# Low parts of 32 weight tiles made in an earlier stage, kept in DRAM and loaded back

## The reference, cut to what matters

```python
def peer_ffn(x, w_q, sub_keys, expert_u, expert_v):
    ...
    def chunk(args):
        xc, ec, gc = args
        a = jnp.einsum('cd,ckd->ck', xc, expert_u[ec])
        w = (gc * jax.nn.gelu(a.astype(jnp.float32))).astype(x.dtype)
        return jnp.einsum('ck,ckd->cd', w, expert_v[ec])
```

## Time and profile before

| | us |
|---|---|
| median of 3 runs | 2193.26 (2191.37 to 2193.62) |
| the profiled execution, device time | 2191.22 |
| its span in the trace | 2189.5 |

### The profile page before, as it was taken

The page is one execution under the profiler, slowest core; times in us unless marked ns, Lnnn a source line. Parts: engine busy times, 40 slices in busy tenths (PEclk is TensorE's granted clock), DMA queues, the critical chain, the costliest instruction groups (busy, mean ns, idle before and its releaser), DMA issues.

```text
span 2189.5 us, 33425 instructions
## 1 busy us (share of the span) xinstructions
PE 2124.8 (97%) x11713; PEld 1787.7 (82%) x11713; DVE 1650.1 (75%) x3228; ACT 1042.0 (48%) x1940; POOL 638.7 (29%) x425
## 2 busy tenths in 40 slices
PE   7999999999999988899999989999999999999999
PEld 6888888888888545687899988999998888888777
DVE  6555555534367687564399999999988989999999
ACT  5333333322243477744455535999844333343332
POOL 0000000000040000020100223777626767777773
PEclk9999999999999999999999999999999999999999
DMA  5322222232234200022355888999989999999997
GB/s 195 97 86 86 86 86 95 80 99 98 98 101 177 77 1 1 1 68 87 125 177 177 279 260 290 382 408 400 392 306 408 419 418 418 418 418 418 411 418 290
DMA packets 137228, 484.57 MB, mean 221 GB/s; under 512 B 15056, under 2 KB 30416, under 8 KB 135184
## 3 DMA queue, kind: packets, MB, share of 16 engines
q1 hardware_dynamic: 75456, 229.93, 30.0%
q0 software_dynamic: 59056, 225.14, 26.1%
q10 hardware_dynamic: 2592, 27.85, 3.1%
HBM read 435.42 MB, written 46.92 MB: 220 GB/s over the span
## 4 chain that ended last, share of the span: by engine, by line
PE 63%; DVE 21%; DMA 10%; ACT 3%; issue 2%; POOL 1%; ACTq 0%; DVEq 0%; POOLq 0%
PE bank L495 15%; PE bank L496 15%; PE bank L497 15%; DMA rows<-peer_v,idxU 9%; PE bank L1257 7%; DVE rows L2327 6%; DVE wlo L482 4%; PE bank L510 2%; DVE own L2332 2%; DVE hot L2485 2%; DVE hot L2483 2%; PE bank L610 1%; PE bank L570 1%; PE bank L813 1%; PE bank L1211 1%
## 5 line engine op out<-in xcount | busy, mean ns | idle before, releaser
L495 PE MATMUL bank<-act_hi,whi 128*128 128x320 f32 (+1 forms) x1840 | 646.4, 351 | 23.2 <-DVE wlo L482 19.8
L496 PE MATMUL bank<-act_lo,whi 128*128 128x320 f32 (+1 forms) x1840 | 635.1, 345 | 0.0
L497 PE MATMUL bank<-act_hi,wlo 128*128 128x320 f32 (+1 forms) x1840 | 634.8, 345 | 0.0
L482 DVE TENSOR_TENSOR wlo<-raw,whi 128x1024 fp32r<-128x1024 f32 x398 | 485.8, 1222 | 141.5 <-ACT whi L478 139.3
L478 ACT ACTIVATE whi<-raw 128x1024 fp32r<-128x1024 f32 x398 | 416.4, 1055 | 262.5 <-PE bank L1257 114.1
L495 PEld LDWEIGHTS bank<-act_hi,whi 128*128 128x128 f32 x1840 | 346.0, 188 | 65.7 <-DVE wlo L482 23.4
L497 PEld LDWEIGHTS bank<-act_hi,wlo 128*128 128x128 f32 x1840 | 345.8, 188 | 32.7
L496 PEld LDWEIGHTS bank<-act_lo,whi 128*128 128x128 f32 x1840 | 346.2, 188 | 31.4 <-issue 0.7
L762 POOL DMA_INDIRECT rows<-peer_u,idxU x128 | 196.7, 1537 | 337.5 <-DVE udot L2327 168.9
L1257 PE MATMUL bank<-whi,h_hi 128*128 128x512 f32 x768 | 238.4, 391 | 7.1 <-DVE wlo L482 4.2
L1257 PE MATMUL bank<-whi,h_lo 128*128 128x512 f32 x768 | 237.4, 390 | 0.0
(11 more groups left out here) (403 smaller groups left out, 2905.6 us busy)
## 6 DMA issues: line engine op xcount, KB each, us to landing
raw<-tiles SPq DMA_DIRECT2D x398, 512.0 KB, 4.9
gates_dram<-stage ACTq DMA_DIRECT2D x12, 2048.0 KB, 11.6
wg<-gates_dram POOLq DMA_DIRECT2D x16, 1536.0 KB, 17.0
acts_dram<-gelu SPq DMA_DIRECT2D x120, 160.0 KB, 5.1
hf<-acts_dram POOLq DMA_DIRECT2D x30, 640.0 KB, 13.6
bias<-alibi POOLq DMA_DIRECT2D x16, 256.0 KB, 2.9
w1s<-cmp_w POOLq DMA_DIRECT2D x1, 4096.0 KB, 13.0
res<-x_t ACTq DMA_DIRECT2D x4, 512.0 KB, 6.9
```

The source lines that it names most:

```text
L482: dve.tensor_tensor(wlo[:, j.slot, :], raw[:, j.slot, :], whi[:, j.slot, :].bitcast(F32), ALU.subtract).then_inc(lo_made, 1)
L495: pe.matmul(to, wh, x, start=(kc == 0), stop=False)
L496: pe.matmul(to, wh, xl, start=False, stop=False)
L497: last = pe.matmul(to, wl, x, start=False, stop=(kc == KC - 1))
```

## The change

32 tiles of the up projection, those of U jobs 36 to 67 (`EARLY_LO`), get an additional job each in the merge stage. That stage goes from 32 to 64 jobs, in groups of four: two of its own (slots 0 and 1) and two of the additional ones (slots 2 and 3). For an additional job SP loads the raw tile, ACT makes the high part, DVE the low part, and SP stores the low part to `lo_dram` in DRAM; nothing is multiplied. DVE counts the job as done once its store has landed (`low_stored`). To keep the count in order, PE waits, ahead of the last chunk of the next group's first product, until the group's stored jobs are counted (`after_stored`).

In stage U DVE makes no low part for jobs 36 to 67: it waits for the high part and for `lo_moved`, and raises `lo_made`. SP loads the low part of job j + 4 right after it has stored the gelu of job j, first waiting until the load two before has landed (two semaphores in turn, so two are under way). It then asks for the raw tile of job j + 8 when the high part of job j + 4 is made, where it waited for its low part before. ACT makes all high parts as before.

Row dots are spread anew: tile 2 from 6 to 12, tile 3 from 18 to 28, gates from 76 to 72, rest from 12 to 18. So 130 uses lie ahead of stage V and 190 in it, where it was 112 and 208. `load_gates(0)` comes after the gather number `SEEN_GATES + ROWS + DOTS_REST // 4`. Some semaphores are renamed or shared.

```diff
-J_C = J_B + 32
+J_C = J_B + 64
...
+EARLY_LO = range(36, 68)
...
-DOTS_TILE = [(0, 0), (0, 0), (6, 10), (18, 0)]
-DOTS_GATES = 76
-DOTS_REST = 12
+DOTS_TILE = [(0, 0), (0, 0), (12, 10), (28, 0)]
+DOTS_GATES = 72
+DOTS_REST = 18
...
+            with sp.Fori(0, J_C // RING - J_B // RING) as i:
+                for m in range(RING):
+                    load(Job(J_B + RING + m, i))
+                    if m >= 2:
+                        sp.dma_start(lo_dram[bass.ds(i * 2 + m - 2, 1), :, :],
+                                     wlo[:, m, :].bitcast(F32)).then_inc(lo_moved[m % 2], 16)
...
-            with sp.Fori(0, U_REST // RING) as i:
+            def store_and_load(i, at_, with_lo):
                 for m in range(RING):
-                    j = Job(J_U + m, i)
+                    j = Job(J_U + at_ + m, i)
                     was_taken(sp, j)
-                    sp.dma_start(acts_dram[bass.ds(i * RING + m, 1), :, :], gelu[:, m, :])\
+                    sp.dma_start(acts_dram[bass.ds(i * RING + at_ + m, 1), :, :], gelu[:, m, :])\
                         .then_inc(acts_stored[m], 16)
-                    load(Job(J_U + 8 + m, i))
+                    if with_lo:
+                        moved = lo_moved[m % 2]
+                        sp.wait_ge(moved, (i * 2 + m // 2 + len(EARLY_LO) // 2) * 16)
+                        sp.dma_start(wlo[:, j.slot, :].bitcast(F32), lo_dram[bass.ds(i * RING + m, 1), :, :])\
+                            .then_inc(moved, 16)
+                        sp.wait_ge(hi_made, Job(J_U + at_ + RING + m, i).n + 1)
+                        into_raw(Job(J_U + at_ + 8 + m, i))
+                    else:
+                        load(Job(J_U + at_ + 8 + m, i))
...
-            for n in range(SEEN_GATES + ROWS + DOTS_REST // 2):
+            for n in range(SEEN_GATES + ROWS + DOTS_REST // 4):
                 gather(n)
...
+            def after_stored(j):
+                def wait(kc):
+                    if kc == KC - 1:
+                        result_of(pe, j)
+                return wait
...
+                    if m % 4 < 2:
+                        if m == 1:
+                            pe.wait_ge(y_split, 2 * KC)
+                        hi, lo = ((act_hi, act_lo), (yc_hi, yc_lo), (act_hi, act_lo), (ya_hi, ya_lo))[m // 4 % 2 * 2 + m % 4]
+                        multiply(pe, j, hi, lo, after_stored(Job(J_B - 1 + m, i, 16)) if m % 4 == 0 else None)
...
+                def low_stored(unit, *stored_jobs):
+                    for moved in lo_moved:
+                        dve.wait_ge(moved, (unit + 1) * 16)
+                    for j in stored_jobs:
+                        dve.wait_ge(taken[j.slot], j.turn + 1)
+                        dve.sem_inc(taken[j.slot], 1)
+                        dve.sem_inc(job_done, 1)
...
             def u_job(n):
-                make_lo(dve, Job(J_U + n).ahead())
+                j = Job(J_U + n).ahead()
+                if n + AHEAD in EARLY_LO:
+                    dve.wait_ge(hi_made, j.n + 1)
+                    at_ = n + AHEAD - EARLY_LO.start
+                    dve.wait_ge(lo_moved[at_ % 2], 16 * (len(EARLY_LO) // 2 + at_ // 2 + 1))
+                    dve.sem_inc(lo_made, 1)
+                else:
+                    make_lo(dve, j)
...
+    early = u[EARLY_LO.start:EARLY_LO.stop].reshape(16, 2, P, D)
+    b = np.concatenate([b.reshape(16, 2, P, D), early], 1).reshape(64, P, D)
```

132 lines of the change are left out of this document (78 added, 54 removed).

## The result

Before: 2192.94 us (median of 4 runs). After: **2242.87 us** (2241.09 to 2243.99, 4 runs), ratio 1.0229 with a 95% interval of 1.0216 to 1.0242. The change costs 50 us. The forecast was 2202, with a range to 2217: the sign was right, the size wrong.

The account below looks back on a forecast made before the run. PE bounds the kernel nearly everywhere, DVE tile 3. Merge stage 0, tiles 2 and 3 +14, gate steps -4.6, rest of U +3, stage V -4 sum to +8.4 us on 2193.26: 2201.7, likeliest 2202, range 2179 to 2217.

Parts of the forecast that it names:

- The gate steps, the rest and stage V: After the tiles: gate steps -4.6 us, rest of U +3, stage V -4, from row dots moved between them.
- The merge stage: 0 was forecast: Merge stage: additional loads, splits and stores cost 0 us, upper end +5, since transfers and DVE have room.
- its store has about 5 us to land, and a raw load lands in 3.4 us here: Merge stage: a group's second store has about 5 us to land, judged by a raw load's 3.4 us.
- DVE waits some 1.3 us per group, which its slack covers: Merge stage: at a loaded queue's landing time of 6.3 us, DVE's wait of 1.3 us per group fits its slack.
- the merge stage longer than 179 us: Merge stage: a sign that would show the forecast wrong; it expected still 174 us.
- Tiles 2 and 3: +14 was forecast: Tiles 2 and 3: 64.6 MB at 418 GB/s take 154.6 us, 9.6 more; with imperfect packing +14, ends -6 and +22.
- its 3.7 us: Start of tiles 2 and 3: 3.7 us of transfers lost because POOL's gathers begin only at 1228.
- at the other end the last jobs have no low load and DVE binds them as now: End of tile 3: DVE, not transfers, binds the last jobs; part of why the term was +14.
- the upper end I had given, +22: Tiles 2 and 3: upper end of the +14 term, if nothing is regained at the end either.
- The first (transfers fit, 0.25): Rival, tiles 2 and 3: low loads and rows find room, over 445 GB/s; total 2179.7 us; chance 0.25.
- The second (they cancel, 0.17): Rival: tiles lose only 3 to 8 us, sum within 3 us of zero, about 2193 us; chance 0.17.
- The third: Rival, jobs 40 to 67: SP's queue gets half the rate, 5.8 us per job, +64 us, 2251.7; chance 0.05.

Follow-up runs that it names:

- Experiment 2: Changed kernel with the low part's store issued ahead of the raw load in the merge stage: 2216.44 us, ratio 1.0112.
- experiment 10, second run: Kernel before plus the merge stage storing 32 low parts, store first, `mg_lo` ahead of the store wait, none loaded back: 2193.06 us, ratio 1.0000.
- experiment 11: Changed kernel with its own dots, store first, `mg_lo` ahead of the store wait, low-load wait on PE: 2210.02 us, ratio 1.0076.
- experiments 4 and 5: Changed kernel with row dots and gates load as before the change: alone 2233.05 us; with the store also ahead of the raw load 2201.60 us.
- experiment 6: Kernel before with only the change's row dots and place of `load_gates(0)`, no low parts stored or loaded: 2203.01 us, ratio 1.0047.
- experiment 13: Mended kernel, dots as before, low loads for jobs 52 to 67 only, first one ahead of the waiting raw load: 2192.28 us; for jobs 56 to 71: 2191.67 us.

## Why the prediction went wrong

**What was right.** That the transfers, not DVE, would bind tiles 2 and 3: 406 to 416 GB/s against the forecast 410 to 420, 20.3 us of PE waits for low loads in small pieces against "some 20 to 30", and 64.6 MB against 64.6 (378 GB/s for 171 us). Halving the loads took 13 us away, halving DVE's work on the dots 2. The gate steps, the rest and stage V were right in kind and size.

**The merge stage: 0 was forecast, 24.2 measured, and 4.8 more behind it.** The step that failed is "its store has about 5 us to land, and a raw load lands in 3.4 us here", with the bound "DVE waits some 1.3 us per group, which its slack covers". The landing time came from a queue in which each load goes out alone. The store goes out behind three raw loads of 512 KB, and takes about 8 us; DVE's wait was up to 5 us in each of 16 groups, 73.2 us in all. Even with the loaded queue's 6.3 us the prediction let slack cover the wait, all but an upper end of +5. But the wait stands in a ring (store, wait, next low parts, next store), and there a wait doesn't hide in slack, it sets the period: 12.6 us instead of 10.9. That DVE would be busy for only 109 of 174 us was no argument: its work was in line behind the wait. The start of stage C, where PE waits 3.9 us for `mg_lo` behind the last of these waits, was in no term. That forecast step also had the test for it, "the merge stage longer than 179 us", and it came out as 193. Experiment 2 removed 27 of the 29.9 us ahead of U's first job with one exchange, and the mended merge stage alone (experiment 10, second run) has U's first job at 1070.2 us as before. Where the store stands in SP's loop is plain in the diff; what stands ahead of it there had no term.

The Trainium skill, DMA: Bandwidth & Descriptors, Anatomy of one DMA, gives for a transfer issued by GpSimd a fixed part of about 2 us plus the bytes at 436 GB/s; for this tile that is 3.2 us, an estimate from that page. Here SP issues the transfer, and its raw load alone comes close (3.4); the store behind three others took about 8 us, so the rule can't be used for a transfer in a filled queue.

**Tiles 2 and 3: +14 was forecast, +25.9 measured.** The step is right but mis-sized at its end. 64.6 MB at the 408 GB/s measured are 158.3 us. The start didn't lose its 3.7 us (393 GB/s in the first window), the end of tile 3 lost more: 29 us at 233 GB/s with DVE busy 28.3, that is 29 x 175 / 408 = 12.4 us of transfers not used. 158.3 + 12.4 = 170.7, and the stretch has 171. This is an account of where the trace's time is, not a proof. My sentence "at the other end the last jobs have no low load and DVE binds them as now" was true, but in the sum I let the saturated part and this tail share the time, though they follow each other. The term should have been near the upper end I had given, +22: the same text says that DVE's freed time can't be saved up. No wait could be mended to save it: with all of them mended (experiment 11) these jobs take 311.7 of 312.9 us, with a shorter tail and a slower start. By what was added, 17 to 18 of the 25.9 us go with the 16 dots (experiments 4 and 5) and the rest with the low loads. The same dots cost 17 us without any low load (experiment 6), through DVE: the place they were moved to had no room in either resource.

**The clock** was in no term. In the last window of the stretch the granted clock is 0.88, in those before it 0.97 to 1.00, where it was 1.00 before, and PE was busy 142.7 us (the sum of the five windows) for work that took 134.7 before: 8 of the 26 us of PE are not idle time but work done more slowly after its waits. This divides PE's time; that the slower work lengthened the stretch, which the transfers and DVE bind, is not shown.

**The rivals.** The first (transfers fit, 0.25) is excluded: it needed 445 GB/s, and no slice of the page was above 418. The second (they cancel, 0.17) needed 3 to 8 us in the tile stretch and is excluded by 25.9. The third priced a job at 5.8 us if SP's queue got half of the rate; measured were 4.9 in the chain from 1296 to 1345, and 4.5 in the mean of jobs 40 to 67. At 1.21 MB per job, 4.9 us is 247 of 416 GB/s, 59%. The Trainium skill (DMA: Bandwidth & Descriptors, Queues, rings and completion order) has each DMA engine go round between the queues that have work. That SP got more than half would fit a POOL queue that is empty at times, but no run here tests it.

**What the change was worth.** By the medians, one edit after the other: 2242.9 to 2216.4 by the order of store and raw load, to 2201.6 by the dots (18 us won in the tiles, 3.5 in the rest of U and 1.5 at the start of C, 5 given back in V and 3 in the gate steps), to 2197.1 by DVE's place in line, to 2196.6 by `mg_lo` (within the noise); the last 4 us need fewer low loads and another order at the seam of SP's loops, and end at no difference. The gain to be had, DVE's 9.3 us of PE waits in tile 3, is used up by the waits that the loads bring with them. What stays open is why jobs 53, 54, 61 and 62 of experiment 13 still take 5.5 us; whether the two-at-a-time rule or the rate of 416 GB/s is behind it wasn't tried.

## What to carry to other kernels

A wait on a transfer that closes a ring must be priced at the landing time of that transfer in its own place in the queue, with everything issued ahead of it; take it from rows with such a queue, not from a lone load, and put what someone waits for first. Before work is moved to transfers, add up the bytes of the stretch and divide by the highest rate seen, then add the stretches in which the other engine binds: phases that follow each other add, they don't overlap. At each seam between two loops of an in-order queue, ask what the first new transfer stands behind.
